# Hybrid attention, pooling, gating and convolution block: the first projections take all eight token tiles per weight step, and the first one takes x without its norms

## The reference, cut to what matters

```python
def rms_norm(x, g):
    return x * lax.rsqrt(jnp.mean(x * x, axis=-1, keepdims=True) + EPS) * g

h = rms_norm(x, norm_g)
(q, k, v, z_a, p_in, z_b, u, v_sgu, z_c, glu_a, glu_b, z_d, merge) = jnp.split(h @ w_in, SPLIT_POINTS, -1)
q = apply_rope(rms_norm(q, q_norm_g), cos, sin)        # 8 heads of 64
k = apply_rope(rms_norm(k, k_norm_g), cos, sin)        # 2 heads of 64
o_c = u * (w_s @ layer_norm(v_sgu) + b_s)              # position mixing, 4 groups of 128 features
...
return x + mixed @ w_out
```

## Time and profile before

| what | value |
|---|---|
| median of 3 runs | 2107.12 us |
| the profiled execution | 2107.21 us, span 2105.4 us |
| TensorE (PE) busy | 2081.7 us, 99% |
| weight loads of TensorE (PEld) | 1720.3 us, 82% |
| GpSimd (POOL) | 1291.1 us, 61% |
| VectorE (DVE) | 1284.6 us, 61% |
| ScalarE (ACT) | 823.1 us, 39% |
| granted TensorE clock, mean | 0.997 |
| moved by DMA | 197.25 MB, mean 94 GB/s |

### The profile page before, as it was taken

How to read it: one execution, slowest core, us unless ns; L and a number is a source line. 1 busy time by engine, 2 the same in 40 slices (tenths; PEclk the granted TensorE clock), 3 DMA queues, 4 the chain that set the end, 5 groups by cost and what they waited for, 6 DMA issues and landing times.

```text
span 2105.4 us, 27266 instructions
## 1 busy us (share of the span) xinstructions
PE 2081.7 (99%) x9772; PEld 1720.3 (82%) x9772; DVE 1284.6 (61%) x1502; ACT 823.1 (39%) x1579; POOL 1291.1 (61%) x987
## 2 busy tenths in 40 slices
PE   6999999999999999999999999999999999999999
PEld 5898877788888888888888887778888888888887
DVE  6875544588878745335378845447888786452331
ACT  5433644334233435324444245443432333443331
POOL 5457544676669767654455665447766696675543
PEclk9999999999999999999999999999999999999999
DMA  5322232312441334414543132323234213434153
GB/s 187 87 68 96 66 116 85 118 53 66 85 96 43 79 77 85 139 55 147 159 129 98 56 104 87 100 86 101 61 80 89 69 51 82 89 71 140 50 200 100
DMA packets 114565, 197.25 MB, mean 94 GB/s; under 512 B 12288, under 2 KB 21760, under 8 KB 114432
## 3 DMA queue, kind: packets, MB, share of 16 engines
q1 hardware_dynamic: 97728, 165.29, 25.7%
q0 software_dynamic: 9216, 16.78, 5.9%
q10 hardware_dynamic: 7488, 13.44, 1.7%
HBM read 153.52 MB, written 41.94 MB: 93 GB/s over the span
## 4 chain that ended last, share of the span: by engine, by line
PE 94%; POOL 2%; DVE 1%; ACT 1%; issue 1%; DMA 0%; DVEq 0%; SPq 0%; POOLq 0%; ACTq 0%
PE acc L639 79%; PE acc L687 6%; PE aux L687 4%; POOL wlo L564 1%; PE aux L759 1%; PE aux L778 1%; PE aux L769 1%; POOL wsum L568 1%; PE aux L722 1%; PE aux L793 1%; PE aux L735 0%; PE aux L800 0%; PE acc L832 0%; DVE pool L1309 0%; ACT prob L1108 0%
## 5 line engine op out<-in xcount | busy, mean ns | idle before, releaser
L564 POOL TENSOR_TENSOR wlo<-raw,whi 128x512 fp32r<-128x512 f32 x464 | 634.2, 1368 | 545.3 <-ACT whi L900 544.6
L639 PE MATMUL acc<-fhi,whi 128*128 128x512 f32 x2048 | 801.7, 391 | 1.9 <-DVE blo L1312 1.9
L639 PE MATMUL acc<-fhi,wlo 128*128 128x512 f32 x2048 | 797.2, 389 | 0.0
L639 PE MATMUL acc<-flo,whi 128*128 128x512 f32 x2048 | 797.0, 389 | 0.0
L900 ACT ACTIVATE whi<-raw 128x512 fp32r<-128x512 f32 x464 | 290.7, 627 | 516.8 <-PE acc L639 383.8
L639 PEld LDWEIGHTS acc<-fhi,whi 128*128 128x128 f32 x2048 | 384.4, 188 | 83.8 <-issue 3.7
L639 PEld LDWEIGHTS acc<-fhi,wlo 128*128 128x128 f32 x2048 | 384.4, 188 | 80.7
L639 PEld LDWEIGHTS acc<-flo,whi 128*128 128x128 f32 x2048 | 384.6, 188 | 78.4 <-issue 0.2
L564 POOL TENSOR_TENSOR wlo<-wsum,whi 128x512 fp32r<-128x512 f32 x192 | 271.1, 1412 | 171.4 <-ACT whi L900 171.0
L1316 DVE SCALAR_TENSOR_TENSOR aux<-conv,allp,aux 128x1024 f32<-128x1024 f32 x232 | 299.1, 1289 | 20.0 <-issue 0.4
L639 PE MATMUL acc<-bhi,whi 128*128 128x512 f32 x512 | 201.8, 394 | 0.0
(11 more groups left out here) (183 smaller groups left out, 2352.3 us busy)
## 6 DMA issues: line engine op xcount, KB each, us to landing
raw<-wstream SPq DMA_DIRECT2D x464, 256.0 KB, 2.7
md<-prev POOLq DMA_DIRECT2D x64, 256.0 KB, 4.2
x<-x SPq DMA_DIRECT2D x32, 256.0 KB, 4.8
md<-prev SPq DMA_DIRECT2D x32, 256.0 KB, 3.6
out<-x ACTq DMA_DIRECT2D x32, 256.0 KB, 2.3
mx<-md SPq DMA_DIRECT2D x24, 256.0 KB, 4.8
qd<-qst ACTq DMA_DIRECT2D x16, 256.0 KB, 2.3
qs<-qd SPq DMA_DIRECT2D x16, 256.0 KB, 2.7
```

Of the source, the lines that this page charges most:

```text
L564: nc.gpsimd.tensor_tensor(wlo[:, f % SLOTS, :], src, whi[:, f % SLOTS, :].bitcast(F32), ALU.subtract).then_inc(lo_made, 1)
L639: mm = nc.tensor.matmul(dst, w, m[:, kt0 + k, cols], start=first and k == 0 and n == 0, stop=last and k == UK - 1 and n == 2, skip_group_c ...
```

## The change

Once per layer instead of twice, each weight step of VS, Q and KV runs over all eight token tiles, first tiles 4 to 7 (PSUM `aux`), then 0 to 3 (`acc`). KV packs its eight tiles into `aux` alone. PLAIN becomes VS (8 steps), Q (8), KV (4): 20 units a layer. VS multiplies x times the norm's gain, without r; v_sgu's variance is multiplied by the square of 1/rms before epsilon is added and the result again by 1/rms. For the VS stage x is split into slots of its own (`X_SLOT`), and h is made while VS runs, block by block, each as soon as its VS step is done. In layer 0 the squares come from rows of x (token-major, a new input, 4 MB), with ScalarE's accumulation; in layer 1 from blocks as before, but summed once for all eight tiles, between the sixth and seventh tile of VS's first step. The norms go from a 128x8 tile to memory and come back as a 128x1024 broadcast, both on ScalarE's queue. The spreads by TensorE and the diagonals go. `form_rest` of the last two forms and the mix of groups 2 and 3 move into the first U pair, both k rotations behind the second; q is copied out of PSUM by ScalarE before it is squared; v_sgu is normalised by ScalarE (16 operations) for VectorE (8).

The core of the diff:

```diff
-WARMUP = 16
+WARMUP = 22
-PLAIN = (("VS0", 8), ("VS1", 8), ("Q1", 8), ("KV1", 4), ("Q0", 8), ("KV0", 4))
+PLAIN = (("VS", 8), ("Q", 8), ("KV", 4))
...
+            for k, tiles in enumerate(((), (0,), (1, 2), (3, 4), (5, 6), (7,), (), ())):
+                load_x(k)
+                for t in tiles:
+                    load_row(t)
...
-            def token_major(L, name, n, t, banks, between=None):
+            def token_major(L, name, n, between=None):
...
+                    if name == "VS":
+                        pe.wait_ge(x_ready, x_turn(L, k, 1) + 1)
+                    if name == "Q":
+                        pe.wait_ge(h_ready, (L * KT + k + 1) * 2)
+                    for n_tile, tile in enumerate((4, 5, 6, 7, 0, 1, 2, 3)):
+                        if name == "VS" and L and k == 0:
+                            if n_tile >= 4:
+                                pe.wait_ge(taken["abcd"[tile]], L * BANK_N["abcd"[tile]])
+                            if n_tile == 6:
+                                token_sums(L)
+                            if n_tile == 7:
+                                pe.wait_ge(rms_root, L + 1)
+                        if name == "Q" and k == 0 and n_tile % 2 == 0:
+                            pe.wait_ge(vs_taken, 8 * L + 2 * (n_tile // 2 + 1))
+                        if name == "KV" and k == 0:
+                            pe.wait_ge(q_taken, 4 * L + 2)
...
-                pe.wait_ge(roped, 6 * L + (1, 2, 4, 5)[n])
+                pe.wait_ge(sgu_taken, 4 * L + 4)
+                pe.wait_ge(roped, 6 * L + (1, 2, 3, 6)[n])
...
+                token_major(L, "VS", 8)
+                token_major(L, "Q", 8)
+                token_major(L, "KV", 4, {0: lambda L=L: row_sums(L), 2: lambda L=L: sgu_mix(L, (0, 1))})
+                pe.wait_ge(sgu_taken, 4 * L + 2)
+                pair(L, "U", 0, {"p7": lambda L=L: sgu_mix(L, (2, 3))})
...
+            def store_norms(L):
+                act.wait_ge(norms_made, L + 1)
+                act.dma_start(rd[L].rearrange("t p -> p t"), rms[:], allow_slow_non_contiguous=True).then_inc(norms_stored, 16)
+            def load_spread(L):
+                act.wait_ge(norms_stored, 16 * (L + 1))
+                act.dma_start(spreads[:], rd[L:L + 1].rearrange("o t p -> o (t p)").partition_broadcast(P)
+                              ).then_inc(spread_loaded, 16)
+            def h_rounded(L, k):
+                act.wait_ge(step_done, stepped(L, "VS", k))
+                for t in range(2):
+                    act.wait_ge(h_scaled, (L * KT + k) * 2 + t + 1)
+                    copy(fhi[H_SLOT[k // UK, t]][:, k % UK, :], x_block(k, t)).then_inc(h_hi, 1)
...
+                if k == 5:
+                    rms_stage(0)
+                if k == 6:
+                    store_norms(0)
...
+                    load_spread(L)
+                    next_high(L, "VS", 4)
+                    for k in range(5):
+                        h_rounded(L, k)
+                next_high(L, "VS", 5)
+                h_rounded(L, 5)
+                next_high(L, "VS", 6)
+                h_rounded(L, 6)
+                act.wait_ge(half_done, 2 * L + 1)
+                take_vs(L, 4)
+                take_vs(L, 6)
+                act.wait_ge(step_done, stepped(L, "VS", 7))
+                take_vs(L, 0)
+                take_vs(L, 2)
...
+            for k in range(KT):
+                if k == 7:
+                    norms(0)
+                for t in range(2):
+                    x_rest(0, k, t)
...
                 for i in range(2):
-                    turns = rotate_steps(L, 4 + i)
+                    turns = rotate_steps(L, 2 + i)
                     sum_x(L, "U", i)
+                    if i == 0:
+                        last_forms()
                     turns[0]()
                     sum_v(L, "U", i)
                     turns[1]()
+                    if i == 0:
+                        last_mixes()
                     sum_22(L, "U", i, BANK_AP["b"])
...
+                    if i:
+                        rotate(L, 4)
+                        rotate(L, 5)
```

More of the change, by code:

```diff
@@ L664, in pair @@
                     mm.then_inc(step_done, 1)
-            def token_major(L, name, n, t, banks, between=None):
+            def token_major(L, name, n, between=None):
+                per = KT // n
+                width = W // per
                 for k in range(n):
@@ L670, in token_major @@
                     pe.wait_ge(lo_made, f + 1)
[L671 to L680, removed]
+                    if name == "VS":
[14 more added lines that the diff above has]
+                            pe.wait_ge(q_taken, 4 * L + 2)
+                        if name == "KV":
+                            dst = aux[:, tile // 4, tile % 4 * width:(tile % 4 + 1) * width]
+                        else:
+                            dst = tile_bank(tile)
                         for e in range(per):
                             kk = k * per + e
-                            s = H_SLOT[kk // UK, t]
-                            at = slice(tile * P, (tile + 1) * P)
+                            s = (X_SLOT if name == "VS" else H_SLOT)[kk // UK, tile // 4]
+                            at = slice(tile % 4 * P, (tile % 4 + 1) * P)
                             w_at = slice(e * width, (e + 1) * width)
@@ L691, in token_major, with token_sums @@
                         between[k]()
[L693 to L700, removed]
+            def token_sums(L):
+                pe.wait_ge(taken["d"], L * BANK_N["d"])
+                pe.wait_ge(xsq_added, 2 * (KT - 1))
+                for n in range(TT):
+                    mm = nc.tensor.matmul(acc[:, 1, HALF + n:HALF + n + 1], sumsq[:, n * P:(n + 1) * P],
@@ L701, in token_sums @@
                                           ones[:, 0:1], start=True, stop=True)
                 mm.then_inc(tok_summed, 1)
[L704 to L708, removed]
             def row_sums(L):
                 pe.wait_ge(bias_made, 2 * L + 1)
-                nc.tensor.matmul(aux[:, 0, HALF:SEQ], ones[:], sgt[:].rearrange("p g i -> p (g i)"),
+                pe.wait_ge(q_taken, 4 * L + 4)
@@ L812, in conv_var, with project_out @@
                 ones_sum(conv[:, WT, PADC:SW], 0, d_var)
-            def project_out(L, t, d, between=None):
+            def project_out(L, t, d):
                 bank = "abcd"[d % 4]
@@ L893, in _ @@
                 for d in range(KT):
-                    hooks = {0: lambda L=L: token_sums(2 * L + 2, 0), 1: lambda L=L: spread(2 * L + 2, 0)}
-                    project_out(L, 1, d, hooks.get(d) if L + 1 < LAYERS else None)
+                    project_out(L, 1, d)
         @block.scalar
@@ new lines, in h_rounded, with take_vs @@
+            def h_rounded(L, k):
[3 more added lines that the diff above has]
+                    copy(fhi[H_SLOT[k // UK, t]][:, k % UK, :], x_block(k, t)).then_inc(h_hi, 1)
+            def take_vs(L, tile):
+                src = (acc, aux)[tile // 4][:, tile % 4 // 2, :].rearrange("p (t g c) -> p t g c", t=2, g=WT)
+                for e in range(2):
+                    copy(vs[e][:, :, tile:tile + 2, :].rearrange("p g t c -> p t g c"), src[:, :, 2 * e:2 * e + 2, :]
+                         ).then_inc(vs_taken, 1)
@@ L1176, in _ @@
                 root(L, 1, 16)
-                for k in range(1, 4):
-                    next_high(L, "KV1", k)
+                square_q(L, 3)
+                root(L, 2, 16)
+                root(L, 3, 16)
+                for k in range(4):
+                    next_high(L, "KV", k)
+                square_k(L, 0)
                 square_k(L, 1)
+                root(L, 4, 8)
+                root(L, 5, 8)
                 form_rounded(L, 6)
                 form_rounded(L, 7)
-                next_high(L, "Q0", 0)
```

479 lines of the change are left out of this document (244 added, 235 removed).

## The result

The changed kernel takes 2112.33 us in the median (2111.53 to 2113.52), the kernel before, measured beside it, 2107.06 us (2105.79 to 2108.38): a ratio of 1.0027, 95% interval 1.0017 to 1.0037. It is slower by 5.3 us, which is little, but the interval leaves out 1. The forecast was 2103 us and faster, and 2112.33 lies a third of a microsecond above the range's end. The profiled execution has a span of 2109.7 us, for 2105.4 before, at a mean granted clock of 0.994.

A forecast was written before the change was run, and what follows sets the result against it. Only TensorE's own work, or a stall of it, was taken to move the time. From 2107.2 us, 16 gained in layer 0 and 2 in layer 1, 13.8 lost in U and ZC, gave 2103 us; range 2089 to 2112.

The forecast's parts named there:

- one wait in U: First U pair, each layer: the rotation's end and first product hold the next pair's p1 by 1.8 us.
- I take 4.0: Layer 0: the store of 1024 single norm values lands after 4.0 us, between nearest rows of 2.3 and 7.8.
- Q's start: Layer 0: Q waits for ScalarE's copy of VS until 58.0, against VS's end at 52.5, a stall of 5.5 us.
- The low clock behind the stall: Layer 0, behind the stall in front of Q: low granted clock costs 1.7 to 1.9 us more.
- the gain of layer 0: U's work in layer 0 stands at 134.6 instead of 150.5: 16 us gained.
- Layer 1: Spreads and sums go, one sum over eight tiles comes: 2.0 us gained; its root costs 0, bounds 0 and 1.5.
- U was put at 2.4 a layer: First U pair: moved form rests and mixes make p4 wait 0.6 and the next p1 1.8 us; bounds 0 and 4.
- The fourth turn: End of second U pair: q's fourth turn waits 3.7 us for both k rotations, plus 0.8 for the clock, each layer.
- D: Rival: the norms' store lands after 7.8 us, leaving a layer 0 gain of 12; 2107 us, chance 0.13.

The follow-up runs named there:

- the runs of the turn: Against the changed kernel, the fourth turn of q waits for rotation 4, not 6; the first load of q for the scores waits for 6: 2100.64 us.
- the mixes moved last: Against the changed kernel, VectorE takes the mixes of groups 2 and 3 in the first U pair after the product that frees bank c: 2108.01 us.
- the mixes moved first: Against the changed kernel, VectorE takes the mixes of groups 2 and 3 behind the sum of p7 in the first U pair: 2112.20 us.
- the early copies: Against the changed kernel, layer 0 only: ScalarE copies VS out of its banks after two steps of h instead of behind seven: 2102.47 us.
- the ordered store: Against the changed kernel, norms stored in 32-byte runs, landing in their own buffer and put in token order by two ScalarE copies: 2107.57 us.

## Why the prediction was wrong, by its steps

The mechanisms were the right ones and in their places, but for one wait in U that didn't come; the forecast fell on sizes, and on one above all.

- **The step that failed is "I take 4.0" for the store of the norms.** It measured 11.36, also beyond the upper bound of 7.8. The reason given, that the bytes are few, was the mistake: the two nearest rows move 64 times the bytes, in 128 pieces each, and landed in 2.3 and 7.8, so they say nothing of a transfer cut into 1024, and neither bounds it. The trace of before held no write of single values. By the Trainium skill (DMA: Bandwidth & Descriptors, Specifications) a write below 512 bytes is a read-modify-write; the run shows more, since runs of 32 bytes are below that too and landed in 1.4 us in layer 1. The bytes of the two stores are the same, so it is the cutting into pieces that is paid: 1024 in 9.4, 128 in 1.4, or 8.9 ns for each of the 896 pieces between them. The number of pieces and their size changed together here; which of the two is paid wasn't tried.
- Q's start was put at 58.0 and came at 66.39, 8.4 later: +7.4 the store, +0.4 the norms (stored at 31.5 for 31.1), -0.7 the broadcast load (3.71 for 4.4), +1.4 the chain from the first scale to Q (19.8 for 18.4). The last is VectorE beside GpSimd: two scales took 1.67 and 1.68 for 0.66. The stall is 10.7 for 5.5, though VS began 1.2 later than forecast, which cost nothing. With the store alone put right, the forecast would have been 2110.4: slower, but inside the range. The low clock and the chain carried it past.
- The low clock behind the stall was put at 1.7. Q's first 24 matmuls took 8.6 us for 5.44, so 3.2. It isn't a fixed price: with this start unchanged it was 1.6 in the runs of the turn (7.06 for the 24 matmuls) and of the mixes moved last (7.04), and 3.1 in that of the mixes moved first, so the forecast's 1.7 came out in some executions.
- Together the gain of layer 0 is 6.4 and not 16. Layer 1 gained 2.8 for 2.0, and its store and its root cost nothing, as forecast.
- U was put at 2.4 a layer and cost 1.46: the wait of 0.6 at p4 was 1.0, and the 1.8 at the next pair's first product did not come, until the mixes were moved and brought it (1.2).
- The fourth turn was put at 3.7 and 0.8 for the clock; it measured 3.56, and 1.6 to 1.9. Its cause was right, and the 11.0 us that its removal gave agree with both terms (10.8). In layer 0 of the runs with the early copies and with the ordered store the low clock behind the same wait cost 3.1 and 2.9.
- The sum with the measured terms: 2107.2 - 6.4 - 2.8 + 13.5 = 2111.5, which is the profiled execution's own time (2111.53), 0.8 under the median. Of the 8.5 us between it and the forecast, 9.6 are the gain of layer 0; layer 1 and the pairs give 1.1 back. Of the rivals D (the store lands late, 2107) was the one that came true, past its own price.
- The range was too narrow above for a plain reason: an operation the trace does not show was bounded by rows of another kind, and D was priced at the end of that bound.

## What to carry to other kernels

Count the pieces of a small transfer, not its bytes, and if the layout must change, change it on an engine that is idle and not in an operand that the busy one reads. Before a wait goes to a slow producer, ask what stands in the queue behind its consumer: moving the copies ahead of the late work was worth 9.2 us with the producer untouched, more than the faster store alone (4.3). A semaphore count two rotations too high (6 for 4) can be a wait on work that nobody needs there; it cost 11.0 us, and the chain of waits called it only "issue".

## What the runs showed that was not expected

- 1024 single values of 4 bytes took 9.3 to 9.4 us to land with little else moving and 11.3 to 12.5 in the busy start; the same 4 KB in 128 runs 1.4 to 2.3 and 5.0 to 5.1.
- A scale on VectorE whose second tensor is read with a step of 32 bytes took 1.05 to 1.13 us in the chain for 0.66, without GpSimd beside it, and 2.06 for 1.67 with it. ScalarE's reordering copies of the same data took 1.18 each for about 0.6.
- What a wait costs beside its length differs. That of 1.0 us cost 0.44 more with the clock at 1.00 around it. Those of 3.6 us, and those in front of Q (9.8 to 15.0 us), came with a fall of the granted clock to 0.50 (1.2 GHz) and cost 1.6 to 3.2 more, with no order by their length. Windows of the changed kernel (read the stretch, PE's busy time behind it, and PEclk, third from the end: us, PE busy (x) PEld DVE ACT POOL, PEclk, DMA share, GB/s) around the wait in front of Q, the first wait in U and the fourth turn:

```profile
59.00:66.00 7.00, 0.00 (x0) 0.00 (x0) 7.00 (x9) 3.66 (x7) 3.19 (x2) 0.50 0.23 73
66.00:71.00 5.00, 4.61 (x11) 3.67 (x12) 3.02 (x6) 4.72 (x10) 0.14 (x1) 0.50 0.01 5
...
158.00:166.00 8.00, 6.95 (x31) 5.25 (x30) 7.38 (x11) 1.71 (x3) 4.52 (x4) 1.00 0.09 33
191.00:195.00 4.00, 0.84 (x4) 0.38 (x2) 3.76 (x9) 1.60 (x3) 1.26 (x1) 1.00 0.17 65
195.00:199.00 4.00, 3.60 (x13) 3.25 (x14) 0.98 (x2) 0.00 (x0) 0.00 (x0) 0.57 0.17 67
199.00:204.00 5.00, 5.00 (x27) 4.13 (x26) 1.00 (x2) 2.24 (x4) 2.23 (x2) 1.00 0.13 50
```

- In front of the first matmul, waits of 1.8, 2.0 and 2.4 us were followed by a clock of 0.50, but waits of 1.5, 1.8 and 2.0 us in three other runs left it at 1.00. What decides between them stays open.
